# Head scores and routing begun in the query stage, gate batches spread over 52 expert blocks

## What is computed

```python
def peer(h, wq, k1, k2, u, v):
    q = (h @ wq).reshape(B, S, H, PEER_QDIM)                      # 8 heads, 256 wide
    s1 = jnp.einsum('bshd,hnd->bshn', q[..., :half], k1)          # scores of 128 keys
    s2 = jnp.einsum('bshd,hnd->bshn', q[..., half:], k2)
    v1, i1 = lax.top_k(s1, K)                                     # K = 16
    v2, i2 = lax.top_k(s2, K)
    cand = (v1[..., :, None] + v2[..., None, :]).reshape(B, S, H, K * K)
    cand_idx = (i1[..., :, None] * PEER_NKEYS + i2[..., None, :]).reshape(B, S, H, K * K)
    top_s, pos = lax.top_k(cand, K)
    experts = jnp.take_along_axis(cand_idx, pos, axis=-1)
    gates = jax.nn.softmax(top_s, axis=-1)
    ...
        act = jax.nn.gelu(jnp.einsum('td,tkd->tk', xc, u[ec]), approximate=False)
        return jnp.einsum('tk,tkd->td', act * gc, v[ec])
```

## Time and profile before

| | us |
|---|---|
| median of three runs | 2265.56 |
| lowest and highest | 2265.02, 2267.21 |
| the profiled execution | 2266.52 |
| its span, first to last instruction | 2264.7 |
| PE busy | 2170.5 (96%) |
| DVE busy | 1667.5 (74%) |
| ACT busy | 1182.8 (52%) |
| POOL busy | 323.6 (14%) |

### The profile page before, as it was taken

How to read it: one execution, slowest core, us unless ns; L and a number is a source line. 1 busy time by engine, 2 the same in 40 slices (tenths; PEclk the granted TensorE clock), 3 DMA queues, 4 the chain that set the end, 5 groups by cost and what they waited for, 6 DMA issues and landing times.

```text
span 2264.7 us, 42446 instructions
## 1 busy us (share of the span) xinstructions
PE 2170.5 (96%) x14844; PEld 1997.2 (88%) x14844; DVE 1667.5 (74%) x3032; ACT 1182.8 (52%) x2051; POOL 323.6 (14%) x260
## 2 busy tenths in 40 slices
PE   3999999999999999999989999999999999999998
PEld 2988989999999988888888898999999999888886
DVE  7877557999777778887664666499987776666665
ACT  2346555544666655544453475555456665554444
POOL 0000000000488700000000000000008883000000
PEclk7999999999999999999999999999999999999999
DMA  7864444555433378787643334455553334555563
GB/s 289 290 221 150 168 150 157 179 184 185 150 120 114 122 278 287 289 291 253 194 167 121 118 121 165 151 185 184 179 175 131 121 113 147 192 192 192 194 194 121
DMA packets 112001, 409.76 MB, mean 181 GB/s; under 512 B 12432, under 2 KB 12944, under 8 KB 111248
## 3 DMA queue, kind: packets, MB, share of 16 engines
q1 hardware_dynamic: 111888, 408.24, 53.4%
HBM read 406.62 MB, written 1.57 MB: 180 GB/s over the span
## 4 chain that ended last, share of the span: by engine, by line
PE 87%; ACT 4%; DVE 4%; POOL 2%; issue 2%; DMA 1%; SPq 0%; ACTq 0%; DVEq 0%
PE ps L1336 31%; PE ps L1052 14%; PE ps L1056 14%; PE ps L1053 14%; PE ps L1315 5%; POOL hot L368 2%; PE ps L1265 1%; PE ps L1196 1%; DVE w_lo L619 1%; PE ps L1104 1%; ACT w_hi L382 1%; ACT hot L547 1%; DMA raw<-in_win 1%; PE ps L1298 1%; ACT hot L541 1%
## 5 line engine op out<-in xcount | busy, mean ns | idle before, releaser
L382 ACT CAST w_hi<-raw 128x1024 fp32r<-128x1024 f32 x664 | 695.0, 1047 | 647.2 <-PE ps L1056 583.2
L619 DVE TENSOR_TENSOR w_lo<-raw,w_hi 128x1024 fp32r<-128x1024 f32 x664 | 811.1, 1222 | 287.2 <-ACT w_hi L382 265.3
L1052 PE MATMUL ps<-h_hi,w_hi 128*128 128x256 f32 x3072 | 767.6, 288 | 1.6 <-ACT big L387 1.4
L1053 PE MATMUL ps<-h_lo,w_hi 128*128 128x256 f32 x3072 | 752.5, 283 | 0.0
L1052 PEld LDWEIGHTS ps<-h_hi,w_hi 128*128 128x128 f32 x3072 | 587.8, 191 | 15.8 <-ACT w_hi L382 7.5
L1053 PEld LDWEIGHTS ps<-h_lo,w_hi 128*128 128x128 f32 x3072 | 588.5, 192 | 0.9 <-issue 0.5
L368 POOL TENSOR_SCALAR hot<-con,rt 128x128 f32<-128x128 f32 x256 | 323.4, 1275 | 1566.0 <-DVE neg L996 1518.0
L1056 PE MATMUL ps<-h_hi,w_lo 128*128 128x256 f32 x3072 | 431.6, 283 | 4.2 <-DVE w_lo L619 4.2
L1056 PEld LDWEIGHTS ps<-h_hi,w_lo 128*128 128x128 f32 x3072 | 396.2, 192 | 5.4 <-DVE w_lo L619 5.4
L553 ACT CAST p_hi<-big 128x256 fp32r (+1 forms) x256 | 103.8, 406 | 343.1 <-PE ps L1336 343.1
L1336 PE MATMUL ps<-w_hi,p_hi 128*128 128x512 f32 x1024 | 274.9, 389 | 0.2
(11 more groups left out here) (176 smaller groups left out, 1613.5 us busy)
## 6 DMA issues: line engine op xcount, KB each, us to landing
raw<-in_u SPq DMA_DIRECT2D x256, 512.0 KB, 3.4
raw<-in_v SPq DMA_DIRECT2D x256, 512.0 KB, 3.5
raw<-in_win SPq DMA_DIRECT2D x104, 512.0 KB, 3.9
hot<-in_ada SPq DMA_DIRECT2D x80, 512.0 KB, 3.5
raw<-in_wq SPq DMA_DIRECT2D x32, 512.0 KB, 4.3
big<-in_ada SPq DMA_DIRECT2D x16, 512.0 KB, 14.8
raw<-in_wout SPq DMA_DIRECT2D x16, 512.0 KB, 3.6
big<-in_decay SPq DMA_DIRECT2D x2, 1536.0 KB, 12.0
```

Of the source, the lines that this page charges most:

```text
L382: nc.scalar.copy(w_hi[:, j % 2, :], raw[:, j, :]).then_inc(hi_ready, 1)
L619: tt(w_lo[:, j % 2, :], raw[:, j, :], w_hi[:, j % 2, :].bitcast(F32), ALU.subtract).then_inc(lo_ready, 1)
L1052: mm(o, w, h_hi[:, k, :], start=(k == 0), stop=False)
L1053: mm(o, w, h_lo[:, k, :], start=False, stop=False)
```

## The change

The scores of two heads (a pair, two groups) are made behind query blocks 5, 9 and 13 and behind expert block 1. ACT copies them in query steps 6, 10 and 14 and in expert step 2. The groups are ordered by head now: group 2p + t holds heads 2p and 2p+1 for tokens of half t, and `unit_at` gives the units in the order in which they become ready. DVE begins with routing in query step 7 (`Q_FIRST`), nine pieces earlier (`N_EARLY` = 16 - 7), and waits at the first piece of each unit for the group it needs. `N_U1` becomes 71, so all that hangs on it comes nine blocks earlier, and the batches are spaced with 50 in place of 42: batch b stands behind block 76 + 50b//32, blocks 76 to 124. `N_PROD` becomes 51.

```diff
 UNIT_BLOCKS = 5
-N_U1 = UNIT_BLOCKS * UNITS
+Q_FIRST = 7
+N_EARLY = N_WQ - Q_FIRST
+N_U1 = UNIT_BLOCKS * UNITS - N_EARLY
 TURN_AT = N_U1 + 2
...
+def unit_at(i):
+    pair, half, one = i // 4, i // 2 % 2, i % 2
+    return PH * half + 2 * pair + one, 2 * pair + half
 def gate_after(b):
-    return G_FIRST + b * 42 // N_GATE
+    return G_FIRST + b * 50 // N_GATE
...
-                stage(l, B_WQ, N_WQ, lambda m: qt[:, ds(m, 1), :], ACT.Copy)
-                for g in range(8):
-                    act.wait_ge(score_ready, 8 * l + g + 1)
-                    nc.scalar.copy(score[:, 2 * g:2 * g + 2, :],
-                                   bank(M[g % 2]).rearrange("p (a n) -> p a n", a=2)).then_inc(score_copied, 1)
+                def copy_scores(pair):
+                    for g in (2 * pair, 2 * pair + 1):
+                        act.wait_ge(score_ready, 8 * l + g + 1)
+                        unit = PH * (g % 2) + 2 * pair
+                        nc.scalar.copy(score[:, unit:unit + 2, :],
+                                       bank(M[g % 2]).rearrange("p (a n) -> p a n", a=2)).then_inc(score_copied, 1)
+                for m in range(N_WQ):
+                    n = l * N_BLOCKS + B_WQ + m
+                    round_hi(n + 2, (m + 2) % RING)
+                    take(n, qt[:, m:m + 1, :], ACT.Copy, m)
+                    if m in (6, 10, 14):
+                        copy_scores((m - 6) // 4)
...
+                    if m == 2:
+                        copy_scores(3)
...
-                for m in range(1, N_WQ):
-                    low(l * N_BLOCKS + B_WQ + m + 1, (B_WQ + m + 1) % RING)
-                dve.wait_ge(score_copied, 8 * (l + 1))
...
-                def unit(i, j):
+                def unit(at, j):
+                    i, group = unit_at(at)
+                    if j == 0:
+                        dve.wait_ge(score_copied, 8 * l + group + 1)
...
+                for m in range(1, N_WQ):
+                    low(l * N_BLOCKS + B_WQ + m + 1, (B_WQ + m + 1) % RING)
+                    if m >= Q_FIRST:
+                        unit((m - Q_FIRST) // UNIT_BLOCKS, (m - Q_FIRST) % UNIT_BLOCKS)
...
-                        unit(m // UNIT_BLOCKS, m % UNIT_BLOCKS)
+                        unit((m + N_EARLY) // UNIT_BLOCKS, (m + N_EARLY) % UNIT_BLOCKS)
...
-                stage(l, B_WQ, 2, N_WQ - 2)
-                pe.wait_ge(keys_in, 16 * (l + 1))
-                pe.wait_ge(out_taken, l * EV + E_U)
...
-                stage(l, B_U, 0, N_U1)
+                def scores(pair):
+                    if pair == 0:
+                        pe.wait_ge(keys_in, 16 * (l + 1))
+                    pe.wait_ge(out_taken, l * EV + E_WQ + 4 * pair + 4)
+                    for g in (2 * pair, 2 * pair + 1):
+                        if g >= 2:
+                            pe.wait_ge(score_copied, 8 * l + g - 1)
+                        for a in range(4):
+                            h, side, t = 2 * pair + a // 2, a % 2, g % 2
+                            last = mm(bank(M[g % 2])[:, P * a:P * (a + 1)], qt[:, 2 * h + side, P * t:P * (t + 1)],
+                                      kt[:, 2 * h + side, :], start=True, stop=True)
+                        last.then_inc(score_ready, 1)
+                for m in range(2, N_WQ):
+                    project(l * N_BLOCKS + B_WQ + m, l * EV + E_WQ + m, m % RING)
+                    if m in (5, 9, 13):
+                        scores((m - 5) // 4)
+                for m in range(2):
+                    project(l * N_BLOCKS + B_U + m, l * EV + E_U + m, m % RING)
+                scores(3)
+                stage(l, B_U, 2, N_U1 - 2)
```

More of the change, by code:

```diff
@@ L387, in take @@
                 nc.scalar.activation(dst, bank(E[j % 2])[:, 0:SEQ], func).then_inc(out_taken, 1)
[L389 to L401, removed]
             act.wait_ge(c_in, 16)
@@ L892, in next8 @@
                     us.done(mi(idx_[:, 8:16], val_[:, 8:16], work))
-                def unit(i, j):
+                def unit(at, j):
+                    i, group = unit_at(at)
+                    if j == 0:
+                        dve.wait_ge(score_copied, 8 * l + group + 1)
                     if j < 2:
                         side = score[:, i, P * j:P * (j + 1)]
-                        if i or j:
+                        if at or j:
                             top8(val[:, j, :], idx[:, j, :], side, s1[:, P * j:P * (j + 1)])
```

## The result

| | us |
|---|---|
| before, median of four runs | 2265.43 (2265.02 to 2267.21) |
| after, median of four runs | 2280.84 (2280.19 to 2281.39) |
| ratio after to before, 95% interval | 1.0066 (1.0049 to 1.0084) |
| profiled execution after, its span | 2280.62, 2278.8 |
| forecast (range) | 2280.0 (2275 to 2286) |

The account below looks back on a forecast made before the run. PE, busy in 96% of the span, was taken as the bound. Stalls +9.6, gate batch 3 -0.5 and scores -2.0 make +7.1 us a layer, +14.3 for two; against the median 2265.56 that gives 2279.8, forecast 2280 (2275 to 2286).

Parts of the forecast that it names:

- Where PE stands still: Gate stretch: PE loses 10.5 us a layer, waiting mostly for ACT's columns; 20.9 us idle before gate batches over both layers.
- The count of the stalls: Gate batches whose preceding block has no batch behind it stall: 17 a layer in place of nine, +9.6 us a layer.
- The price of a stall: At a stalled gate batch PE loses 1.20 us, 0.98 idle and 0.22 starting up again.
- The lower bound: Smallest price of a stall at a gate batch: the bare idle time, 0.97 us.
- Why ACT is late: Gate stretch: ACT's columns queue behind a rounding awaiting a finished block; the pass takes 3.76 us, one block covers 2.88.
- POOL and gate 3: Gate stretch: POOL's columns stay hidden, gate batch 3's wait goes (-0.5 us a layer), the first batch's 1.39 us wait stays.
- Head scores: Scores moved between query and expert blocks no longer wait for ACT's last result: -2.0 us a layer, bounds 0 and 2.0.
- Routing moved beside the query blocks: Nine routing pieces move to query steps on idle DVE; PE had not waited for them, so nothing gained on PE.
- Spreading cures the stalls: Rival for the gate stretch: spread batches find all columns ready, -13.3 us a layer, 2239 us; chance 0.07.
- Part of the stalls only: Rival for the gate stretch: ACT's pass is hidden at some new two-block steps, 2259 or 2268 us; chance 0.05.
- stalling scores: Rival for the query stage: each of four score groups waits as the one group did, +15.0 us a layer, 2296; chance 0.05.
- late routing: Rival: DVE waits for copied scores, so expert blocks wait for `low`, 1.7 to 3.4 us a layer, 2283 to 2287; chance 0.03.

Follow-up runs that it names:

- early columns: Changed kernel, but ACT writes its three columns of a batch one step earlier where the preceding block has no batch: 2238.90 us; with old spacing too, 2240.74 us.
- old spacing: Changed kernel with gate batches spaced by b*42//32 in place of b*50//32, all else as changed: 2262.21 us, ratio 0.9983 to the kernel before.
- The two kernels with other column counts: Changed kernel with two columns on ACT and two on DVE: 2258.68 us; changed kernel with four on ACT and three on POOL: 2305.14 us.
- the kernel without gaps: Changed kernel with a gate batch behind each of 32 consecutive blocks (76 to 107): 2275.11 us, ratio 1.0039 to the kernel before.

## Why the prediction was right, point by point

**Where PE stands still.** The reading from the table of stretches and the list of waits held. Work on PE did not change: between the two traces its idle time before the gate batches grew by 15.2 us, that before the scores fell by 3.1, and its busy time grew by 2.3 with the new starts. That makes 14.4 us; the spans differ by 2278.8 - 2264.7 = 14.1, and 14.3 were forecast. The medians differ by 15.4.

**The count of the stalls.** Seventeen a layer, as counted from `gate_after`: 34 waits in the trace, and 18, 14 and 0 where the experiments left 18, 14 and 0 gaps in ACT's cover. The idle time before the gate line, forecast near 37 us, is 36.1. This was the step that decided the sign.

**The price of a stall.** 1.20 us forecast, of which 0.98 idle; 5.88 - 4.66 = 1.22 measured in the changed trace, and by difference of times 41.9 / 34 = 1.23 (early columns), (18.6 + 1.0) / 16 = 1.23 (old spacing, with the 1.0 us that the prediction gives gate 3). The lower bound, bare idle time, would have been too low by a fifth: PE needs its new start as well.

**Why ACT is late.** Less load could not bring its pass forward, since it starts from idle. The two kernels with other column counts show it from both sides, and the one with early columns removes it. By the Trainium skill, "TensorE: Matmul & The Clock Gate", in the section "Architectural detail" (on queue depths), ScalarE's queue is strictly first in, first out; the trace agrees, as the columns stayed behind the rounding through 3.33 us of idle time, and of the experiments only those that changed ACT's own list moved them.

**POOL and gate 3.** POOL stayed hidden, and gate 3's wait went: of POOL's waits only the first of each layer is left. That wait, 1.38 us, stayed, as said.

**Head scores.** Four groups of 16 records with nothing waited for. The low parts (line 1064) around one of them in the timeline of PE:

```profile
340.67 1.12 PE L1064 MATMUL ps<-h_hi,w_lo 128*128 128x256 f32 x8
341.63 1.95 PE L1306 MATMUL ps<-big 128*128 128x128 f32 x16
345.33 1.12 PE L1064 MATMUL ps<-h_hi,w_lo 128*128 128x256 f32 x8
```

340.67 to 345.33 is 4.66 us, a block and 1.78, and so it is around the other three groups of the layer: the whole 1.96 us came off, not a part. The gain was forecast at 3.9 us for both layers and measured at 3.3 (old spacing in the changed kernel against the kernel before) and 4.3 (the same with early columns).

**Routing moved beside the query blocks.** No gain and no loss on PE. The copies on ACT took 1.06 us in a step with 1.6 us free, and the next rounding found 0.59 of it left:

```profile
321.18 1.06 ACT L522 COPY big<-ps 128x512 f32<-128x512 f32 x2
322.83 1.05 ACT L390 CAST w_hi<-raw 128x1024 fp32r<-128x1024 f32 x1 [0.59 <-PE ps L1064]
```

DVE's first piece started at 322.17, right behind its `low` of 321.03, so the new wait for copied scores cost nothing. From the scores to the end of the expert stage PE waits for `w_lo` once a layer, at the softmax, 1.68 us as before.

**The rivals.** Spreading cures the stalls: no, it nearly doubled their number; the 2239 us that this rival gave is what the kernel reaches when the condition named for it, columns written before the rounding, is made true (2238.9). Part of the stalls only, stalling scores, and late routing: none of them showed. The change did do what it says. It spread the batches and gave POOL 112 us of waiting in place of 48.

**Left open.** Why POOL's four columns take from 3.1 to 7.1 us is not tried here; the kernel without gaps shows only that it makes a bound. In the changed kernel's trace the four columns begun at 641.35 took 3.14 us, with DVE idle from 642.84 on, and those begun at 646.00 took 7.14 with DVE at work nearly throughout, which points to DVE and proves nothing. The softmax wait was not tried either.

## What to carry to other kernels

An engine that works through its list in order, and stands idle at a wait, delivers the work behind that wait at a fixed time after the event that ends it (3.76 us here), so look at what covers that time at each place, not at the engine's mean load: spreading the consumers out can uncover it. Count the places, take the price from start to start rather than from the idle time, and try moving the producer's instructions ahead of the one that waits, which added no work here. When a wait behind another has been removed, ask again whether the same rule applies to it.

## What the runs showed of the hardware

PE loses about 0.22 us more than its idle time at each stall: 34 stalls of 0.97 us idle cost 41.9 us. Two parts of it can be read in the rows above. The 16 records of a batch took 2.02 us behind a stall and 1.95 without one (590.25 and 594.99). And a batch that need not wait starts 0.96 us after the start of the low part before it (594.03 to 594.99), though that part is modelled as 1.12 us long, so 0.16 us of overlap is lost too.

Two waits in the changed kernel and one in the kernel before are put down to DVE. The first two are gone where only ACT's list was changed. The instruction named there belongs to the next batch and ended just as PE began, 700.41 + 1.22 = 701.63, and ACT's last column ended at 701.35:

```profile
700.41 1.22 DVE L948 TENSOR_TENSOR hot<-rt,con 128x1024 f32<-128x1024 f32 x1
...
701.63 2.02 PE L1331 MATMUL ps<-hot 128*128 128x128 f32 x16 [1.00 <-DVE hot L948]
```

A column of 128x128 on POOL took 0.78 us at the least and 3.08 at the most, by this row of the changed kernel (least, median, most, in ns; what makes the long ones is not shown):

```profile
L376 POOL TENSOR_SCALAR hot<-con,rt x256: 782/792/3075, 569.8 to 1895.0; 128x128 f32<-128x128 f32 x128
```
